# A decoder trunk with routed experts: the expert loop's place in an instruction block, and when GpSimd adds the early rows

## The reference

```python
logits = (xt @ w_router).astype(jnp.float32)
top_logit, top_idx = lax.top_k(logits, TOP_K)            # 2 of 8 experts for each token
gates = jax.nn.softmax(top_logit, axis=-1)
...
hid = jax.nn.silu(xb @ w_gate[e]) * (xb @ w_up[e])       # 1024 -> 3584
return hid @ w_down[e]                                   # 3584 -> 1024
...
y = jnp.zeros((T, D)).at[row_tok].add(yb * row_g[:, None])
```

## Time and profile before

| | us |
|---|---|
| median of 3 runs | 1325.47 (1324.51 to 1325.51) |
| profiled execution | 1328.43 |
| its span | 1326.6 |
| PE busy in the span | 1290.7 |
| DVE / ACT / POOL busy | 677.4 / 252.0 / 63.7 |

### The profile page before, as it was taken

The page is one execution under the profiler, slowest core; times in us unless marked ns, Lnnn a source line. Parts: engine busy times, 40 slices in busy tenths (PEclk is TensorE's granted clock), DMA queues, the critical chain, the costliest instruction groups (busy, mean ns, idle before and its releaser), DMA issues.

```text
span 1326.6 us, 38823 instructions
## 1 busy us (share of the span) xinstructions
PE 1290.7 (97%) x17222; PEld 1007.6 (76%) x17222; DVE 677.4 (51%) x943; ACT 252.0 (19%) x386; POOL 63.7 (5%) x50
## 2 busy tenths in 40 slices
PE   9999999999999999999999999999999999999898
PEld 9998899988767567567766955866875695696597
DVE  5875655554875556165145335516614614542661
ACT  5564544443643100000000000000000000000000
POOL 1001000000000330000000000000000000002600
PEclk9999999999999899999999999999999999999999
DMA  9867565565522999999999999999999999999992
GB/s 320 261 213 227 187 191 181 180 223 179 186 93 72 388 419 418 416 419 417 416 418 417 416 416 410 417 417 409 417 416 405 417 416 402 417 417 416 405 398 103
DMA packets 114224, 442.93 MB, mean 334 GB/s; under 512 B 9284, under 2 KB 55700, under 8 KB 83348
## 3 DMA queue, kind: packets, MB, share of 16 engines
q1 hardware_dynamic: 107904, 424.75, 81.3%
q10 hardware_dynamic: 4820, 11.53, 2.5%
q0 software_dynamic: 1344, 4.20, 0.8%
HBM read 434.12 MB, written 12.08 MB: 336 GB/s over the span
## 4 chain that ended last, share of the span: by engine, by line
PE 90%; DVE 4%; ACT 3%; issue 3%; DMA 0%; ACTq 0%; DVEq 0%
PE bank L2003 22%; PE bank L2051 22%; PE bank L2021 20%; PE bank L1553 7%; PE bank L1555 7%; PE bank L1554 7%; ACT w_hi L661 1%; DVE w_lo L955 1%; PE bank L1800 1%; PE bank L1711 1%; DMA const<-in_shape_constants 0%; PE bank L1976 0%; ACT ht_hi L689 0%; DVE sums L1478 0%; PE bank L1855 0%
## 5 line engine op out<-in xcount | busy, mean ns | idle before, releaser
L2003 PE MATMUL bank<-raw,xT 128*32 128x384 f32 (+1 forms) x2688 | 260.5, 532 | 10.7 <-issue 9.8
L2003 PEld LDWEIGHTS bank<-raw,xT 128*32 128x32 f32 x2688 | 110.8, 110 | 154.3 <-issue 133.8
L2021 PE MATMUL bank<-more_ring,xT 128*32 128x256 f32 (+1 forms) x3072 | 207.0, 354 | 0.4 <-issue 0.4
L955 DVE TENSOR_TENSOR w_lo<-raw,w_hi 128x2048 fp32r<-128x2048 f32 x62 | 141.4, 2289 | 98.0 <-ACT w_hi L661 98.0
L1473 DVE TENSOR_TENSOR sums<-more_ring 128x768 f32<-128x768 f32 (+1 forms) x64 | 69.8, 1090 | 234.3 <-PE bank L2021 193.3
L2051 PE MATMUL bank<-more_ring,hidT 128*32 128x256 f32 x3072 | 170.7, 379 | 0.0
L2021 PEld LDWEIGHTS bank<-more_ring,xT 128*32 128x32 f32 x3072 | 147.4, 110 | 25.2 <-issue 5.0
L2051 PEld LDWEIGHTS bank<-more_ring,hidT 128*32 128x32 f32 x3072 | 150.4, 110 | 18.1
L1553 PE MATMUL bank<-ht_hi,w_hi 128*128 128x256 f32 x464 | 128.7, 277 | 1.5 <-DVE ht_lo L969 1.5
L2051 PE MATMUL bank<-raw,hidT 128*32 128x256 f32 x2304 | 129.2, 379 | 0.0
L1555 PE MATMUL bank<-ht_hi,w_lo 128*128 128x256 f32 x464 | 128.3, 277 | 0.0
(11 more groups left out here) (312 smaller groups left out, 1603.1 us busy)
## 6 DMA issues: line engine op xcount, KB each, us to landing
more_ring<-in_moe_w_up SPq DMA_DIRECT2D x64, 1024.0 KB, 17.4
more_ring<-in_moe_w_down SPq DMA_DIRECT2D x64, 1024.0 KB, 16.2
raw<-in_moe_w_gate SPq DMA_DIRECT2D x64, 768.0 KB, 18.3
more_ring<-in_moe_w_up SPq DMA_DIRECT2D x64, 768.0 KB, 18.2
raw<-in_moe_w_gate SPq DMA_DIRECT2D x48, 1024.0 KB
raw<-in_moe_w_down SPq DMA_DIRECT2D x48, 1024.0 KB, 18.9
more_ring<-in_moe_w_gate SPq DMA_DIRECT2D x16, 1024.0 KB
raw<-in_hgrn_w_in SPq DMA_DIRECT2D x15, 1024.0 KB, 11.8
```

Of the source, the lines that this page charges most:

```text
L955: nc.vector.tensor_tensor(w_lo[:, slot, :], raw[:, slot_raw, :], plain(w_hi[:, slot, :]), SUB).then_inc(split_ready, 1)
L2003: ins = nc.tensor.matmul(out_banks[j][GTOK * c:GTOK * c + GTOK, 0:w], xT[:, j, kt, :], chunk[:, c], start=kt == 0, stop=kt == KT - 1)
L2021: ins = nc.tensor.matmul(dst[GTOK * c:GTOK * c + GTOK, :], rows, columns[:, c], start=opens, stop=pair == PAIRS - 1, skip_group_check=True)
```

## The change

PE's loop head stands at slot 0 of an instruction block in place of slot 128. And GpSimd, which has issued its four indirect DMAs, waits for the last item's hidT to be complete (all six groups) before the first multiplication. n_before is the number of items less one.

```diff
-LOOP_SLOT = 128
+LOOP_SLOT = 0
...
                 for i in range(2):
                     at = bass.IndirectOffsetOnAxis(ap=early_slot[:, t, i:i + 1], axis=0)
                     nc.gpsimd.indirect_dma_start(out=early[i][:, t, :], out_offset=None, in_=slot_rows, in_offset=at).then_inc(fetched[t][i], 16)
+            pool.wait_ge(hidT_ready, n_before * (2 * GRPS) + 2 * GRPS)
+            pool.sem_inc(pool_pace, 1)
             for i in range(2):
                 for t in range(TT):
                     pool.wait_ge(fetched[t][i], 16)
```

## The result

The changed kernel takes 1330.58 us (median of 20 runs, 1324.59 to 1333.57); the kernel before took 1326.01 beside it (20 runs). The ratio is 1.0028, with a 95% interval of 1.0016 to 1.0039: slower by 0.3%, not faster by 0.6%, and outside the range. The profiled execution took 1331.24 us, its span 1329.4.

What follows compares the result with a forecast made beforehand. PE, busy 1290.7 of 1326.6 us, ends an item, with the DMA engines full too. PE's 9.8 + 6.2 = 16.0 was capped by transfers at 9.2, less 1.2 behind the loop: 8.0 off 1325.47, so 1317.5 us, range 1311 to 1322.

Steps and rivals of the forecast that it cites:

- The edge: From an item's last down product to the next item's first up product: PE's gap of some 1.35 us goes to zero.
- (c): Rival: the gap between items stays, the branch fetching its target at whatever slot; only 6.2 us saved, 1319.3 us; chance 0.15.
- (d): Rival: the branch stands just behind a block's start, so the gap between items grows to 4.2 us; 1339 us; chance 0.08.
- ACT's copy: At L2079, PE's wait for yb: 24 matmuls, 2.0 us, cover the copy's end 1.42 us after the down products.
- It is worth 9.8 us: Closing the loop-head gap: seven edges of some 1.35 us and two gaps of 0.2 behind block 1.
- It costs nothing at the end as long as the transfers, and not PE, set the last item: At the loop's start: the head's block comes late, 3 us taken, but adds nothing to the total.
- entering the loop: At the loop's start: the head's block may come late by 0 to 5.9 us, 3 taken.
- Part 2: Last item: GpSimd's eight operations wait for hidT, which removes 6.2 us of PE's time, 1.7 of it by the clock.
- Leaving the loop: Behind the loop, within L2114's matmuls: a block crossing costs 1.2 us, bounds 0 to 4.5.
- Part 3: Last item: weight landings stay where they are, so PE moves forward by 9.0 to 9.5 us at most, 9.2 taken.
- PE's gain: What PE alone would win from the loop head and GpSimd's wait: 9.8 + 6.2 = 16.0 us.
- the transfers' room: Last item: load 25 lands 10.3 us ahead of its use, 9.5 at the last pair; 9.2 us taken.

Runs made afterwards that it cites:

- the plain up phase: Changed kernel with the first part's up phase done without the seven-product scheme (192 matmuls of 384 columns for 352 of 192): 1325.18 us, ratio 0.9985 to the kernel before.
- the adds alone: Kernel before plus only GpSimd's wait, loop head left at slot 128: 1320.41 us, ratio 0.9956; once more 1321.0 us, ratio 0.9964.
- four narrow products: GpSimd's wait with the head at slot 128, and four of fourteen down loads multiplied at half width, loads unchanged: 1317.21 us, ratio 0.9929 to the kernel before.

## Why the prediction was wrong

**The edge: right, and worth more than said.** 128 instructions from the head to the next block, 14 transfers an item (138 in all where the earlier trace rows had 15 an item and the page 144), 243 instructions ahead of the branch, the branch at 0.36 us: all as worked out. The prices at 51, 115, 147, 179 and 243 instructions in the last block (3.1, 1.2, 0.5, 0.15 and less than nothing) follow its rule, 5.8 us less 27 ns for each and less 1.6 of queue, within 0.4 us: 2.8, 1.1, 0.2 and then nothing. At slot 0 the branch is through in 0.36 us, where a block that has to be waited for needs 5.8: ahead of the second item the transfer of the head's block runs from 556.02 to 557.08, and the branch, 0.39 us long, starts at 559.2. Rivals (c) and (d) fell with that, and ACT's copy stayed covered.

**The step that failed: "It is worth 9.8 us".** It looked at the boundary before the branch, at the first one of the body and at the one behind the loop, and moved the others, those within the fast phases, without a word: the term for them is nothing, and they took 12.1 us. At slot 128 the item's boundaries lie at instructions 128, 384, 640, 896 and 1152; at slot 0 they lie at 256, 512, 768 and 1024. The first fast phase runs from about 390 to 1100. Both numbers were there to be read. The chain of the third item before has:
```profile
678.59 14.29 PE bank L2021 x344
```
344 matmuls with their loads in 14.3 us are 20.8 ns an instruction, 5.3 us a block, and a block needed 5.8. In the chain above the two blocks are there 6.4 us apart (584.64 and 591.05). So each boundary in such a phase adds half a microsecond or more of lag.

At slot 128 the first boundary falls just ahead of the phase, behind gate products of 83 ns each, of which a block's 128 last 10.6 us (an estimate, 128 x 83 ns). The transfers show this head start: in the second item before, the one for the block at 640 starts 2.4 us behind the first weight load of the block before it (571.41 for 568.99), in the changed kernel the one for 768 starts 4.0 us behind (582.23 for 578.24). From there on each block at slot 128 comes just in time: the blocks at 640, 896 and 1152 are used 2.0, 1.1 and 1.6 us after they landed, where 1.3 to 1.6 is what the late blocks of slot 0 show, and the last stands behind the end of the phase, where the weight loads pause for 0.36 us (ahead of 586.67) and the chain above has no gap of PE from 584.73 to 590.22. At slot 0 the lag shows as 1.6 us an item.

The second fast phase, of 256 columns, takes 6.9 us a block (256 x 27 ns), and no gap of over 0.3 us that waits for a block stands in it in any of these kernels. That the fetch is outrun in the first, in 15 gaps of 12.7 us, is shown by the plain up phase, which had no gap there, and by the landings.

**"It costs nothing at the end as long as the transfers, and not PE, set the last item"**, of entering the loop. The price lay within the bounds, 0 to 5.9, but nearer their far end than the 3 taken: from the start of the branch to the first product 6.2 us pass where 1.5 did, 4.7 more (0.9 of the branch lies beside a wait for xT that was there before; the other 0.9 of the 5.6 in the account had come about ahead of the branch, which starts at 442.92 for 442.04). The price is paid in full, and more goes with it: some 1.5 us of the first item, where the half clock lasts on (its 1.1 are 1.8 won at the edge, 1.4 more in gaps, and this), and the transfers themselves. They were treated as a clock of their own. But up to the entry they have filled the ring, and what they carry from there on is tied to PE's first products: 3.4 us of idle engines, 3.7 us at load 25. A bound that moves with PE's start can't cover a late start.

**Part 2: right in size.** 6.2 us were forecast, and the adds alone save 5.7 in the last item. But the largest piece of the old loss, the 2.8 us in the earlier trace rows, was a late block as well: it stood at instruction 896 and ended at 1236.42, 1.6 us after a transfer of instructions had landed (1234.80). With the adds moved there is no gap; why they made that block late was not settled. The eight ended 1310.5 (forecast 1310 to 1316); the sum L1480 of the last item stayed at 0.95, where the earlier trace rows has 3.13. Of the 6.2, the forecast put 1.7 down to the clock: that is half of the 3.4 us at 0.50 in the earlier trace rows, and in the last item of the changed kernel the clock stays at 1.00 (it does from 454.9 to 1325.3 us).

**Leaving the loop.** 1.2 us taken, within 0 to 4.5; the gap is 1.9, and the stretch behind the last item is 2.5 longer. The clock, again at half for 6.2 us from 1325.3, is in it. The DMA engines, which the forecast had idle there, were at a share of 0.16 from 1320 to 1321 us and at 0.96 from 1321 to 1322, while the block came in 1.56 us.

**Part 3: the mechanism right, not reached.** With the adds alone, and with four narrow products, the landings stay within 1.3 us of where they were and PE moves up to them: 9.0 us (1318.2 to 1309.2) with 0.2 us of room left, and 10.6 to 11.7 where it waits for them. Of the 9.0, 3.2 stood ahead of the last item already (1201.66 for 1204.91), where these two kernels do the same: that is the spread between executions. The term was 9.0 to 9.5: 1 to 2 too small. In the changed kernel the room was never under 5.6 us, because PE was late. The forecast took the lesser of PE's gain and the transfers' room, the second, and the first had shrunk from 16.0 to below nothing.

In sum for PE, forecast and found: edges -9.8 for -12.4 (seven of 1.7, and two gaps of 0.2), boundaries in the fast phase 0 for +12.1 (15 gaps of 12.7, less 0.6 that the first item had), entry 0 for +5.6 and 1.5 of the clock, leaving +1.2 for +2.5, adds -6.2 for -6.1 (4.2 and the last item's new gaps of 1.9). The found ones add up to +3.2, where the spans differ by 2.8.

## What to carry to other kernels

Moving a loop within its instruction blocks moves every boundary of the body, and the way in and out as well as the branch. For each, compare how long the instructions of the block ahead last with what a block needs (here 5.8 to 6.4 us), and keep the phases that issue fastest from holding several in a row. The stream of weights here, which waits for room in a ring, was no independent bound: PE's first product came 5.6 us later, and load 25 of the last item landed 3.7 us later. And of two changes sent together, try each alone: here one is worth 0.4% and the other gives back more than that.

## What the runs showed of the hardware

A block of instructions that PE waits for in the loop comes 5.8 to 6.4 us after the one before was entered, beside full DMA engines (a share of 1.01 in the earlier trace rows). Only 0.9 to 1.1 us of it are the transfer (up to 1.4 with the longer tail): some 3.4 to 4.0 pass before it starts, and 1.2 to 1.9 between its landing and PE's next product. A semaphore increment on PE lasts 51 ns in the trace but comes every 0.15 us, in a row of 120. The branch into a loop whose head begins a block took 5.9 to 6.7 us, with 64 more instructions ahead of it 2.5, and with 120 more 0.3; it was 0.2 to 0.3 where the head stood at slots 64, 128 or 160. A block crossed behind the loop, where the DMA engines had been at a share of 0.00 from 1317 to 1320 us, still cost 1.9 us; its transfer (1320.92 to 1322.48, beside a share of 0.96 from 1321 to 1322) landed 1.35 us before PE went on. And the stretch at a granted clock of 0.50 around the entry lasted 17.1 us in all three kernels in which PE stood still for 5.5 us or more there, and 3.4 to 10.2 in those where the branch took 0.2 to 0.3 us at slots 64, 128 and 160.

At slots 64, 128 and 160 a transfer starts 1.5 to 4.2 us behind the entry's branch too. So a transfer about as late is there at every slot; but the head's block is already in, this is the next one, and PE needs it 96 to 192 instructions later. What sets the moment at which it is asked for stays open.
